# A two-layer conformer and attention trunk on one core: the second layer's first modulation moved into the key projection, LayerNorm weights loaded as columns, convolution rows loaded behind x

## The reference, cut to what matters

```python
c_act = silu(c)
for l in range(2):
    sh1, sc1, g1, sh2, sc2, g2 = split(c_act @ w_ada[l] + b_ada[l], 6)
    h = x * (1 + sc1) + sh1
    if l == 0:                       # conformer: h @ w_pw1, gate, 31-tap convolution,
        y = conformer_conv(h, ...)   # LayerNorm, silu, @ w_pw2
    else:
        shift, scale = split(c_act @ w_ada_kv + b_ada_kv, 2)
        hk = x * (1 + scale) + shift          # keys, values, forget gates from hk
        k, v, f = split(hk @ w_kvf)
        y = fox_attention(h @ w_q, k, v, f) @ w_o
    x = layer_norm(ALPHA * x + (1 + g1) * y, ln_mix_g[l], ln_mix_b[l])
    h = x * (1 + sc2) + sh2
    y = grouped_moe(h, ...)          # 2 of 16 experts for each token
    x = layer_norm(ALPHA * x + (1 + g2) * y, ln_ffn_g[l], ln_ffn_b[l])
```

## Time and profile before

| | |
|---|---|
| median of 3 runs | 1337.11 us (1335.74 to 1339.91) |
| profiled execution | 1337.69 us, span 1336.0 us |
| PE busy | 1141.4 us, 85% of the span |
| DVE, ACT, GpSimd busy | 335.1, 185.5, 23.1 us |
| DMA | 495.70 MB, mean 371 GB/s |
| chain that ended last | PE 58%, DMA 37%, DVE 3% of the span |
| mean granted PE clock | 0.919 of full |

### The profile page before, as it was taken

How to read it: one execution, slowest core, us unless ns; L and a number is a source line. 1 busy time by engine, 2 the same in 40 slices (tenths; PEclk the granted TensorE clock), 3 DMA queues, 4 the chain that set the end, 5 groups by cost and what they waited for, 6 DMA issues and landing times.

```text
span 1336.0 us, 16386 instructions
## 1 busy us (share of the span) xinstructions
PE 1141.4 (85%) x6446; PEld 490.0 (37%) x6446; DVE 335.1 (25%) x760; ACT 185.5 (14%) x333; POOL 23.1 (2%) x68
## 2 busy tenths in 40 slices
PE   6599999868999789676879999988899979985686
PEld 3466454213333223222265754442233322321222
DVE  1078633211211111111150153431212121111113
ACT  0011402101111000011011032210111011100001
POOL 2100000000000000000000000000000000000000
PEclk9799988889999889888989999888899988998888
DMA  9969856999999999999995343799999999999993
GB/s 391 398 235 403 353 214 280 427 427 425 428 426 424 427 426 426 427 427 424 421 418 220 126 190 126 290 409 426 429 425 427 408 426 426 427 426 425 427 427 154
DMA packets 43966, 495.70 MB, mean 371 GB/s; under 512 B 4555, under 2 KB 4571, under 8 KB 9571
## 3 DMA queue, kind: packets, MB, share of 16 engines
q1 hardware_dynamic: 42576, 490.75, 88.0%
q10 hardware_dynamic: 690, 2.34, 0.4%
q0 software_dynamic: 608, 1.21, 0.3%
HBM read 493.23 MB, written 1.05 MB: 370 GB/s over the span
## 4 chain that ended last, share of the span: by engine, by line
PE 58%; DMA 37%; DVE 3%; issue 2%; SPq 0%; ACT 0%; ACTq 0%; POOLq 0%; DVEq 0%
DMA ring<-in_w_up_dram 17%; DMA ring<-in_w_down_dram 9%; PE PS L1053 8%; PE PS L1009 8%; PE PS L870 6%; PE PS L1035 5%; PE PS L887 4%; PE PS L1160 4%; DMA work<-in_w_up_dram 3%; PE PS L1077 3%; DMA ring<-in_w_gate_dram 3%; PE PS L967 3%; PE PS L785 3%; PE PS L994 3%; DMA work<-in_conv_ln_b_dram 2%
## 5 line engine op out<-in xcount | busy, mean ns | idle before, releaser
L1053 PE MATMUL PS<-ring,work 128*32 128x512 f32 x1184 | 162.8, 700 | 79.1 <-DMA ring<-in_w_up_dram 59.5
L1009 PE MATMUL PS<-ring,work 128*64 128x512 f32 x640 | 151.2, 622 | 19.4 <-DMA ring<-in_w_gate_dram 16.1
L1053 PEld LDWEIGHTS PS<-ring,work 128*32 128x32 f32 x1184 | 44.2, 125 | 192.7 <-issue 190.9
L1608 DVE TENSOR_TENSOR work<-work,PS 64x512 f32<-64x512 f32 x23 | 15.9, 692 | 317.2 <-ACT work L622 317.2
L1009 PEld LDWEIGHTS PS<-ring,work 128*64 128x64 f32 x640 | 47.1, 142 | 121.8 <-issue 110.3
L870 PE MATMUL PS<-ring,work 128*128 128x512 f32 x192 | 83.1, 593 | 0.0
L1053 PE MATMUL PS<-work 128*32 128x512 f32 x216 | 47.3, 779 | 33.0 <-DMA work<-in_w_up_dram 23.3
L994 PE MATMUL PS<-work 64*128 64x512 f32 x296 | 73.5, 615 | 1.6 <-DVE work L1585 1.6
L622 ACT ACTIVATE work<-PS 64x512 f32<-64x512 f32 x23 | 13.5, 588 | 434.0 <-PE PS L1053 434.0
L967 PE MATMUL PS<-hs,colv 128*64 128x512 f32 x296 | 72.2, 609 | 0.0
L1035 PE MATMUL PS<-ring,work 128*64 128x512 f32 x320 | 70.9, 595 | 0.1
(11 more groups left out here) (280 smaller groups left out, 997.2 us busy)
## 6 DMA issues: line engine op xcount, KB each, us to landing
ring<-in_w_gate_dram SPq DMA_DIRECT2D x52, 2048.0 KB, 36.4
ring<-in_w_up_dram SPq DMA_DIRECT2D x52, 2048.0 KB, 39.5
ring<-in_w_down_dram SPq DMA_DIRECT2D x52, 2048.0 KB, 32.5
ring<-in_w_ada_dram SPq DMA_DIRECT2D x24, 2048.0 KB, 13.6
work<-in_w_gate_dram SPq DMA_DIRECT2D x12, 2048.0 KB, 29.2
ring<-in_w_pw_dram SPq DMA_DIRECT2D x6, 2048.0 KB, 32.8
xs<-in_w_up_dram SPq DMA_DIRECT2D x12, 1024.0 KB, 29.7
work<-in_w_up_dram SPq DMA_DIRECT2D x12, 1024.0 KB, 32.7
```

The costliest lines, as they stand in the source:

```text
L1009: last = pe.matmul(PS[LARGE * half:LARGE * (half + 1), bank, :], XT[:, kk, LARGE * h:LARGE * (h + 1)], columns(tile, kk, half), start=(h = ...
L1053: last = pe.matmul(PS[SMALL * strip:SMALL * (strip + 1), GATE_BANK, :], XT[:, kk, LARGE * h:LARGE * h + SMALL], columns(load + 2 * h + str ...
```

## The change

- The four tiles of the second layer's first modulation (`L_ADA1_G0`) come between WK and WV in SP's order, instead of ahead of the first experts. PE multiplies them after four of K's eight chunks, and turns them after six. `hTq` is first copied without modulation, and scaled and shifted in place afterwards (`query_columns` on DVE, a loop on ACT).
- The slots ahead of the first experts are handed on in the order in which PE lets go of them (`passed_on` and `sorted`).
- The key-value ada tiles move: the first behind the variance, the next two into `columns_and_turn`, the last into the router, whose gate rows now lie in banks 4 and 7. DVE adds their bias in the router.
- The LayerNorm weights come as columns, by 8 DMAs on ACT's queue, ahead of two rows for the end; `turn_ln` and its copies go.
- The convolution rows are asked for right behind x; PE turns them after the third ada tile, and spreads the taps ahead of the gated product. `keep_busy` is (2, 2, 1, 1) instead of (2, 3, 3, 1) and one more.
- `DVE_STEPS` is written anew; the count of taps is the same.

```diff
@@ order of tiles
-    L_ADA1_G0 = L_PW2 + 2
-    L_MOE0 = L_ADA1_G0 + ADA_G
+    L_MOE0 = L_PW2 + 2
     L_WK = L_MOE0 + 6 * E
-    L_WV = L_WK + 2
+    L_ADA1_G0 = L_WK + 2
+    L_WV = L_ADA1_G0 + ADA_G
...
+        if i == L_MOE0:
+            waiting = collections.deque(sorted(waiting, key=lambda s: passed_on.index(last_in[s])))
@@ DVE
-        DVE_STEPS = (("u", 0), ("conv", (0,), (1,), 2), ("u", 1), ("conv", (0, 1), (3, 1), 3), ("u", 2),
-                     ("conv", (0, 1), (6, 4), 8), ("u", 3), ("conv", (0, 1), (14, 12), 10), ("u", 4),
-                     ("conv", (0, 1), (24, 22), 7), ("conv", (1, 2), (29, 1), 2), ("conv", (2, 3), (3, 1), 3), ("u", 5),
-                     ("ada", 1, 0), ("conv", (2, 3), (6, 4), 10), ("u", 6), ("conv", (2, 3), (16, 14), 9), ("u", 7),
-                     ("ada", 2, 1), ("conv", (2, 3), (25, 23), 6), ("conv", (3, 4), (29, 1), 2), ("conv", (4,), (3,), 28))
+        DVE_STEPS = (("u", 0), ("conv", (0,), (1,), 2), ("u", 1), ("conv", (0,), (3,), 1), ("conv", (0, 1), (4, 1), 2),
+                     ("u", 2), ("conv", (0, 1), (6, 3), 11), ("u", 3), ("conv", (0, 1), (17, 14), 12), ("u", 4),
+                     ("conv", (0, 1), (29, 26), 2), ("conv", (1, 2), (28, 1), 3), ("conv", (2, 3), (4, 1), 8), ("u", 5),
+                     ("ada", 1, 0), ("conv", (2, 3), (12, 9), 12), ("u", 6), ("conv", (2, 3), (24, 21), 7),
+                     ("conv", (3, 4), (28, 1), 3), ("u", 7), ("ada", 2, 1), ("conv", (4,), (4,), 27))
@@ ACT's queue
             for t in range(TT):
                 act.dma_start(hs[:, t, :], x[0, t * P:(t + 1) * P, :]).then_inc(x_in, 16)
-            act.wait_ge(mods_zeroed, 4)
+            for r, w in ((0, w_dw[0, :, 0, :]), (ROW_BA, b_pw1.rearrange("o (r d) -> (o r) d", r=2)), (ROW_BDW, b_dw),
+                         (ROW_LNG, conv_ln_g), (ROW_LNB, conv_ln_b)):
+                act.dma_start(colrows[r:r + w.shape[0], :], w).then_inc(colrows_in, 16)
+            act.wait_ge(mods_zeroed, 3)
...
-            act.wait_ge(landed[home[L_ADA0_G0 + 2]], 16)
-            for r, w in ((0, w_dw[0, :, 0, :]), (ROW_BA, b_pw1.rearrange("o (r d) -> (o r) d", r=2)), (ROW_BDW, b_dw),
-                         (ROW_LNG, conv_ln_g), (ROW_LNB, conv_ln_b)):
-                act.dma_start(colrows[r:r + w.shape[0], :], w).then_inc(colrows_in, 16)
...
-            for r, w in enumerate((ln_mix_g, ln_mix_b, ln_ffn_g, ln_ffn_b)):
-                act.dma_start(lnrows[32 * r:32 * r + 1, :], w[0:1, :]).then_inc(rows_in[0], 16)
+            for l in range(DEPTH):
+                for r, w in enumerate((ln_mix_g, ln_mix_b, ln_ffn_g, ln_ffn_b)):
+                    act.dma_start(ln_cols[l][:, r, :].rearrange("p (h k) -> p h k", h=2),
+                                  w[l].rearrange("(h p k) -> p h k", h=2, k=KH)).then_inc(ln_cols_in, 16)
+            for r, w in ((2, ln_ffn_g), (3, ln_ffn_b)):
+                act.dma_start(lnrows[32 * r:32 * r + 1, :], w[1:2, :]).then_inc(rows_in, 16)
             act.activation(rstd[:, 0:1], eps[:, 0:1], ACT.Sigmoid)
@@ PE, start
+            for j in range(ADA_G):
+                ada_load(L_ADA0_G0, j, 0)
+                if j == 2:
+                    turn_colrows()
+                keep_busy((2, 2, 1, 1)[j])
...
+            spread_taps()
             pe.wait_ge(in_cols_copied, 1)
@@ PE, means and variance
-            ada_load(L_ADAKV, 0, 6)
-            ada_load(L_ADAKV, 1, 6)
             mean(7)
...
-            ada_load(L_ADAKV, 2, 6)
-            ada_load(L_ADAKV, 3, 6)
+            ada_load(L_ADAKV, 0, 6)
@@ PE, columns_and_turn and moe, first layer
+                    ada_load(L_ADAKV, 1, 6)
+                    ada_load(L_ADAKV, 2, 6)
...
-                    ada_load(L_ADA1_G0, 0, B_GATE)
-                    turn_ln(0, 7)
...
-                    for j in range(1, ADA_G):
-                        ada_load(L_ADA1_G0, j, B_GATE)
+                    ada_load(L_ADAKV, 3, 6)
...
+                pe.wait_ge(ada_added, (4, 7)[l])
                 sum_x(first)
@@ PE, keys
-            project_T(L_WK, 0, k_done, hT)
+            project_T(L_WK, 0, k_done, hT, range(KH))
             pe.wait_ge(hTq_copied, 4)
+            ada(L_ADA1_G0, 4)
+            project_T(L_WK, 0, k_done, hT, range(KH, KH + 2))
+            pe.wait_ge(ada_added, 5)
+            turn_mod(modv[1], (0,), TURNED_MODS, 5).then_inc(q_cols_turned, 1)
+            project_T(L_WK, 0, k_done, hT, range(KH + 2, KD))
+            pe.wait_ge(q_cols_ready, 1)
             project(L_WV, 4, v_done)
@@ DVE, router
+                if l == 0:
+                    add_ada(modkv, 0, 6)
                 dve.wait_ge(pos_done, l + 1)
```

More of the change, by code:

```diff
@@ L71, in layer_of, with tiles @@
         return next((l for l, first in enumerate((L_MOE0, L_MOE1)) if first <= i < first + 6 * E), None)
+    def tiles(first, n):
+        return list(range(first, first + n))
+    passed_on = (tiles(L_ADA0_G0, ADA_G) + tiles(L_ADA0_G1, 2 * ADA_G) + tiles(L_PW1, 4) + tiles(L_ADAKV, 1)
+                 + tiles(L_PW2, 2) + tiles(L_ADAKV + 1, ADA_G - 1) + tiles(L_WK, 1) + tiles(L_ADA1_G0, ADA_G)
+                 + tiles(L_WK + 1, 1) + tiles(L_WV, L_MOE1 - L_WV))
     home, earlier, visit, opens = [], [], [], {}
@@ L158, in trunk_kernel @@
         rstd = sb("rstd", [P, TT])
-        ln_cols = [sb(f"ln_cols{l}", [P, KD, 4]) for l in range(DEPTH)]
-        kv_cols = colv[:, 0, 0:32]
+        ln_cols = [sb(f"ln_cols{l}", [P, 4, KD]) for l in range(DEPTH)]
+        kv_cols = colv[:, 0, 0:16]
         cols = sb("cols", [P, 6, KD])
-        TURNED_MODS, TURNED_LN = 0, 64
+        TURNED_MODS = 0
         SCALE, SHIFT, Q_SCALE, Q_SHIFT, RES_SCALE, RES_SHIFT = range(6)
@@ L253, in trunk_kernel @@
         x_in = sem("x_in")
-        rows_in = [sem(f"rows_in{l}") for l in range(DEPTH)]
+        rows_in = sem("rows_in")
         x_done = sem("x_done")
@@ L602, in moe @@
                     r = LARGE * h
-                    last = act.activation(gate_rows[r:r + LARGE, :], PS[r:r + LARGE, 6 + h, :], ACT.Copy)
+                    last = act.activation(gate_rows[r:r + LARGE, :], PS[r:r + LARGE, GATE_ROWS[h], :], ACT.Copy)
                 last.then_inc(gate_copied, 1)
@@ L705, in _ @@
             take_hT(hT, RES_SCALE, RES_SHIFT, 4, hT_copied)
-            take_hT(hTq, Q_SCALE, Q_SHIFT, 4, hTq_copied)
+            for b in (0, 2):
+                act.activation(hTq[:, 2 * b:2 * b + 2, :], PS[:, 4 + b, :].rearrange("p (k t) -> p k t", k=2),
+                               ACT.Copy).then_inc(hTq_copied, 1)
             turned[0] += 1
+            act.wait_ge(q_cols_ready, 1)
+            for b in (0, 2):
+                for k in (2 * b, 2 * b + 1):
+                    last = act.activation(hTq[:, k, :], hTq[:, k, :], ACT.Identity, scale=cols[:, Q_SCALE, k:k + 1],
+                                          bias=cols[:, Q_SHIFT, k:k + 1])
+                last.then_inc(hTq_ready, 1)
             for b in range(4):
@@ L833, in turn_mod @@
                 return last
[L835 to L842, removed]
             hs_turned = [0]
@@ L854, in turn_h @@
                                                 hs[:, t, k * P:(k + 1) * P], ident[:, :])
+                            if t == k == 0:
+                                behind(last)
                         if t == TT - 1:
@@ L942, in moe @@
                     r, v = mod_row(modv[l], 5)(h)
-                    last = pe.matmul(PS[:, 6 + h, :], ones[r:r + 1, :], v, start=True, stop=True)
+                    last = pe.matmul(PS[:, GATE_ROWS[h], :], ones[r:r + 1, :], v, start=True, stop=True)
                 last.then_inc(gate_spread, 1)
                 if l == 0:
-                    for j in range(1, ADA_G):
-                        ada_load(L_ADA1_G0, j, B_GATE)
+                    ada_load(L_ADAKV, 3, 6)
                 pe.wait_ge(xT_copied, 4 * (l + 1))
@@ L1130, in keep_busy @@
                     pe.matmul(PS[:, 2, :], ident[:, :], hs[:, i % TT, 0:BANK], start=True, stop=True)
-            for j in range(ADA_G):
-                ada_load(L_ADA0_G0, j, 0)
-                keep_busy((2, 3, 3, 1)[j])
-            pe.wait_ge(ada_added, 1)
-            turn_mod(modv[0], (0,), TURNED_MODS, 1).then_inc(in_cols_turned, 1)
             def turn_colrows():
@@ L1717, in _ @@
             take_hT(hT, RES_SCALE, RES_SHIFT, 4, hT_copied)
-            take_hT(hTq, Q_SCALE, Q_SHIFT, 4, hTq_copied)
+            for b in (1, 3):
+                dve.tensor_copy(hTq[:, 2 * b:2 * b + 2, :],
+                                PS[:, 4 + b, :].rearrange("p (k t) -> p k t", k=2)).then_inc(hTq_copied, 1)
             hT_turned[0] += 1
```

92 lines of the change are left out of this document (42 added, 50 removed).

## The result

The changed kernel takes **1341.48 us** (median of 6 runs, 1340.46 to 1343.2), the kernel before 1337.06 (6 runs, 1335.51 to 1339.91): ratio 1.0033, 95% interval 1.0019 to 1.0048, slower by 4.4 us. The prediction said 1341. The profiled execution took 1343.2 us (span 1341.4), 1.7 above its median, so its sum comes out larger than the median's.

A forecast was written before the change was run, and what follows sets the result against it. MoE stages were taken as bound by weight arrival, the stretches before the experts and from the key projection to the second MoE stage by PE and DVE; +4.5 - 1.3 - 5.2 - 2.9 + 9.1 = +4.2 on 1337.1 gave 1341, range 1323 to 1346.

The forecast's parts named there:

- Start: Before the first `u`: convolution rows in at 28 us instead of awaited until 53.32; taken alone, 11 us won.
- 1.2 GHz: At the gated product: PE running part of it at this clock would put the first `u` at 59.5, not 57.
- ACT held: Ahead of ACT's sigmoids: issuing column loads stalls it until 73 to 74 us; first `u` at 75, 4.5 us later.
- The count of 136: Column loads on ACT's queue: 8 DMAs give each DMA engine 136 items, 16 pieces and a semaphore write per DMA.
- the drain: ACT's ring on the busiest engine: items go at 0.63 to 0.65 us each up to 53 us, then 0.31 to 0.32.
- the limit: DMA issue: returns when some 70 to 80 items per engine stand ahead; 77 used for ACT's last issue.
- The first rival: No stall on ACT, by deeper room or by packets: first `u` at 57 to 59.5, 1323.5 to 1326 us; chance 0.30.
- -1.3 - 5.2 - 2.9: First `u` to keys: 1.3 us won up to the means, 5.2 from moved ada loads through the router, 2.9 in the ring.
- Key projection: Between K and V: four ada loads and a turn add 9.1 us on PE, with no wait for their tiles.
- the sum +4.2: Whole kernel: all terms together make it 4.2 us slower, 1341 us.
- its own case: ACT held by the column loads, first `u` at 75: 1336 to 1344 us; chance 0.32.
- rival 3: Same ACT stall with a limit of 60 items or 0.35 us a turn: 5 us more, 1346 us; chance 0.25.

The follow-up runs named there:

- experiment 1: Changed kernel with its eight column loads and the two `lnrows` loads issued late by GpSimd instead of ACT: 1325.52 us, ratio 0.9915 to the kernel before.
- experiment 2: Changed kernel with the first layer's four column loads left early on ACT, the other six loads issued late by GpSimd: 1326.22 us.
- experiment 3: Kernel before with the convolution rows asked for behind x and turned after the third ada tile, `keep_busy` four matmuls shorter: 1331.97 us, ratio 0.9964.
- experiment 8: experiment 1 plus, at the column loads' old place on ACT, eight loads of the same vectors as plain 4 KB rows: 1326.14 us.
- experiment 7: Changed kernel with three more column loads behind the eight, to a place nobody reads: 1340.65 us.
- experiment 12: Changed kernel, column loads early, plus 24 small matmuls at PE's start: 1339.87 us, ratio 1.0016 to the kernel before.
- Experiment 5: experiment 3 plus four small matmuls at PE's start, making PE's program as long as in the kernel before: 1323.66 us, ratio 0.9891 to the kernel before.
- experiment 9: experiment 1 plus 24 small matmuls at PE's start: 1322.88 us.
- Experiment 4: experiment 1 with the convolution rows' loads and turns where the kernel before had them, and its longer `keep_busy`: 1340.34 us.
- experiment 10: experiment 1 plus 6 small matmuls at PE's start: 1333.88 us.
- experiment 6: experiment 1 plus 14 small matmuls (7 and 7) at PE's start: 1332.93 us.
- experiment 11: Kernel before with four fewer matmuls in `keep_busy` and nothing else: 1341.3 us, ratio 1.0038.

## Why the prediction was right

**Start.** The rows by 28 us: they were in before PE asked for them at 29.23. The last ada tile "slips to about 32": 32.54. The packet times it is worked out from are in the trace of the kernel before: from 10 to 50 us a weight packet of 16 KB took 0.62 us (median), one of 8 KB 0.31 and a row's of 4 KB 0.16. The gated product from 38.5: 38.97. Without a stall `u` at 57 to 59.5: 59.8, 58.6, 57.2 in experiments 1 to 3. The prediction's "1.2 GHz" stands for the granted clock of 0.50 in the earlier trace rows; no trace gives a clock in GHz.

**ACT held.** The step on which the sign hung. "A last issue at 73 to 74 and the first `u` at 75": 72.3 and 74.3. (By its own terms, 73 to 74 and 2.2, the first `u` would have been at 75.2 to 76.2.) The way there was right in both factors. Experiments 1, 2 and 8 show a threshold in loads that come in pieces. The count of 136 holds: ACT's queue moved 2,862 packets in the kernel after and 682 in experiment 1, which lacks the eight column loads and two rows of 2 packets each; that makes 272 for a load, and three more in experiment 7 make 3,678. By the sizes in the trace, of the kernel after, a load is 256 packets of 16 bytes and 16 semaphore writes of 4 bytes, 17 for each of 16 engines if shared evenly; the last engine shows just that, 16 of the one, then one of the other. For the drain, the DMA view of the kernel after from 47 to 66 us, and from 70.5 to 74.5, when one engine alone had still weights and pieces (q1 is SP's queue, q10 ACT's):

```profile
q1 hardware_dynamic: 968, 7.59, 97.3%
q10 hardware_dynamic: 968, 0.04, 3.5%
```

```profile
q1 hardware_dynamic: 13, 0.11, 6.3%
q10 hardware_dynamic: 13, 0.00, 0.2%
```

As many of one as of the other, and in the second stretch they alternate, 13 pairs in 4.0 us: each piece of 16 bytes, and each 4-byte semaphore write, waits for one weight packet, 0.31 us a pair on each engine, where the prediction had 0.31 to 0.32. For the limit, the packets that this last engine had still to move, counted from its end (75.4 us), were 75 ahead of the eighth load as its issue returned at 69.09, and 82 ahead of the next DMA as that returned at 72.01; the prediction took 77. It is the fullest engine that counts: the others moved their pieces of the eighth load within 1.1 us of that return. A plain count isn't all of it: the seventh load's issue returned in 0.49 us with some 95 ahead (an estimate, at 0.31 us each back from there), and so did two of experiment 7. That is open. The first rival had two ways to an ACT that isn't held, deeper room or packets. For the second the pieces would have to go several at a time; in these stretches one went for one weight packet, a column load took 13 to 23 us (median 18.8) from issue to landing, and ACT was held.

**From `u` to the key projection.** Predicted -1.3 - 5.2 - 2.9, a key projection 4.9 us ahead; measured 4.5 ahead. In parts: 77.2 us instead of the predicted 77.7 from `u` to the means; `sum_x` 2.1 us ahead, predicted 2.0.

**Key projection.** Predicted +9.1, measured +7.2. The four loads and the turn took 8.9, priced at 9.1. But the 128 records of the keys' own matmuls took 28.4 us, not 29.65. Before, the granted clock was 0.50 from 676.0 to 686.2 us, over the first keys; after, it was so from 672.6 to 676.1 and at 1.00 again before the keys.

**Behind V.** The prediction had nothing here, and the profiled execution loses 2.7 us more: 2.7 behind at V, 5.4 at the end of the span. Two rows stand for it: `turn_h` for the second experts, 3.65 instead of 2.39 us, since it now falls behind the drop of the granted clock to 0.50 (at 860.4 us after, 860.3 before), and the hole, 2.6 us; 1.2 of the two come back later. So the sum +4.2 came out near the measured +4.4 by two errors that cancel: 1.9 too much for the keys, and a term of 1.6 (experiment 12 against the change, uncertain by some 2) to 2.6 that was left out, because no row that the prediction read has it. Two smaller misses cancel as well: the first `u` came 3.8 us later and not 4.5, and from there to the keys 8.3 us were won and not 9.4. That the forecast met the median to half a microsecond is luck; the sign is not, but it hung on the held ACT, to which the prediction gave 0.32 in its own case and 0.25 in rival 3.

Between kernels whose first experts have no hole the picture is simple. Experiment 5 against before: the early rows bring 13.4 us. Experiment 9 against 5: the new order, with the longer key projection, brings 0.8 us (by the prediction's terms 0.3), no more than noise: against the kernel before the two ratios are 0.9907 (0.9875 to 0.9939) and 0.9891 (0.9876 to 0.9906). Experiment 4, where the order was to be seen alone, wasn't run without its holes. Experiment 12 against 9: ACT's stall costs 17.0. That makes 2.8 slower, and with the holes 4.4. Without the held ACT, which was the first rival, the change is worth 0.9% (ratios of experiments 1 and 9: 0.9915 and 0.9907).

## What to carry to other kernels

Loads in many small pieces are not free because they are few bytes: beside full weight traffic count their pieces per DMA engine, semaphore writes among them. Here each cost one turn of 0.31 us, and with some 70 to 80 ahead (by the two issues of SP in the earlier trace rows and two of ACT above) the engine that issued mostly waited, and so did all its work behind. Give them to an engine that has nothing due, or load rows and turn them. And where PE's timeline has idle stretches of some us put down to "issue", try a few matmuls more or less ahead of them before you believe a difference under 1%: here four of them were worth 4.6 and 8.3 us.

## What the runs showed of the hardware that was not expected

First, PE's holes look like waits for its own program. In all seven holes that I followed (two each of the kernel after and of experiment 10, one each of 3, 6 and 11), a packet of a DMA queue named "instruction" ends 1.3 to 1.9 us before PE goes on. So it is nearly everywhere: the fourteen traces have 157 stretches of over 0.9 us, from 195 us on, that are put down to "issue", and for 149 of them such a packet, of 16,384 bytes, ends 1.2 to 2.6 us before PE goes on. The DMA view (packets, MB, share of 16 engines) of experiment 10 from 201.8 to 207.6, its hole of 5.92 us, and of experiment 9 from 201.4 to 204.4, within the same gate matmuls (201.45 to 205.09), where PE doesn't stop:

```profile
q1 hardware_dynamic: 166, 2.46, 99.6%
q8 instruction: 1, 0.02, 1.0%
```

```profile
q1 hardware_dynamic: 88, 1.28, 100.2%
```

The packet takes 1.0 us and starts at 205.16, 3.4 us after PE fell silent, with the weights filling the engines (99.6%). In the changed kernel's second stage it is there from 886.80 to 887.76, and PE goes on at 889.17; without a hole, in experiment 9, it starts at 861.23, while PE still runs `sum_x`. In that kernel's first stage packets start at 194.58, ahead of `sum_x`, and at 204.45, amid the gate matmuls, and PE stops for neither. That the late packet is the cause is read from these times and from the fixed place in the program; that it is late because of the weight traffic was not tried. The "instruction" queue moved 80 packets of 16,384 bytes in the kernel after, 1.31 MB in all. In the experts' code holes are up to 9.0 us long (experiment 6). That code stands behind branches, but the holes lie at a counted place amid the gate matmuls as well; whether the branches have a part in them, no run tells.

Second, its size. The time of one and the same kernel moves by 11 us with the length of PE's program alone (1322.9 to 1333.9, experiments 9 and 10), more than twice what separates this change from none.
